# Attention's first scores and exponentials put ahead of the last in-projection block, and the gate's modulation one step later

## What is computed

```python
mod = jax.nn.silu(c) @ w_mod[l] + b_mod[l]
shift, scale, gate = jnp.split(mod, 3, axis=-1)
u = rms_norm(h, norm_w[l]) * (1.0 + scale[:, None, :]) + shift[:, None, :]
p = u @ w_in[l]
q, k, v = qk_heads(p, q_norm_w[l], k_norm_w[l])      # 8 query heads, 2 key heads of 64
k_all = jnp.concatenate([k_c, k], axis=1)            # 256 keys of the context and 512 own
attn = attend_blocked(q, k_all, v_all) * jax.nn.silu(p[..., ZA_LO:ZA_HI])
conv = conformer_conv(p[..., GLU_LO:GLU_HI], ...) * jax.nn.silu(p[..., ZC_LO:ZC_HI])
out = jnp.concatenate([attn, conv], axis=-1) @ w_out[l]
h = h + gate[:, None, :] * out
```

## Time and profile before

| | |
|---|---|
| median of 3 runs | 1076.65 us (1076.53 to 1078.28) |
| the profiled execution, its own time | 1075.98 us |
| its span, first to last instruction | 1074.2 us |
| TensorE matmul (PE) busy | 1041.7 us, 97% |
| VectorE (DVE) busy | 650.7 us, 61% |
| ScalarE (ACT) busy | 455.0 us, 42% |
| granted TensorE clock | 1.000 |
| chain that ended last | PE 76%, DVE 14%, ACT 4%, issue 3%, DMA 2% |

### The profile page before, as it was taken

How to read it: one execution, slowest core, us unless ns; L and a number is a source line. 1 busy time by engine, 2 the same in 40 slices (tenths; PEclk the granted TensorE clock), 3 DMA queues, 4 the chain that set the end, 5 groups by cost and what they waited for, 6 DMA issues and landing times.

```text
span 1074.2 us, 22576 instructions
## 1 busy us (share of the span) xinstructions
PE 1041.7 (97%) x9816; PEld 824.2 (77%) x9816; DVE 650.7 (61%) x1019; ACT 455.0 (42%) x738; POOL 5.6 (1%) x10
## 2 busy tenths in 40 slices
PE   8999998988999999999999999999999999999998
PEld 6777776776787777777777767787888888888887
DVE  4569898975457575868787757664443223444322
ACT  5354554677425543444535245344342112443111
POOL 0000000000000000000000000000000000000000
PEclk9999999999999999999999999999999999999999
DMA  9912134000522210101110121333323232333230
GB/s 362 371 60 98 59 99 174 4 2 2 196 79 99 79 41 22 42 28 37 42 41 23 42 81 42 105 111 98 97 93 105 98 98 79 98 98 105 96 104 30
DMA packets 26161, 95.01 MB, mean 88 GB/s; under 512 B 2896, under 2 KB 3152, under 8 KB 25552
## 3 DMA queue, kind: packets, MB, share of 16 engines
q1 hardware_dynamic: 26064, 93.57, 25.2%
HBM read 89.36 MB, written 4.19 MB: 87 GB/s over the span
## 4 chain that ended last, share of the span: by engine, by line
PE 76%; DVE 14%; ACT 4%; issue 3%; DMA 2%; SPq 1%; POOL 0%; ACTq 0%; DVEq 0%
PE psum L845 20%; PE psum L847 18%; PE psum L846 18%; DVE work L2037 4%; PE psum L855 3%; PE psum L1284 2%; DMA ring<-weights 2%; PE psum L1297 2%; PE psum L1053 1%; DVE small_temps L2226 1%; PE psum L1356 1%; PE psum L1333 1%; PE psum L1009 1%; PE psum L1376 1%; DVE in_weights_low L2093 1%
## 5 line engine op out<-in xcount | busy, mean ns | idle before, releaser
L2093 DVE TENSOR_TENSOR weights_low<-ring,weights_high 128x1024 fp32r<-128x1024 f32 x70 | 85.8, 1226 | 75.3 <-ACT weights_high L1647 75.3
L1647 ACT ACTIVATE weights_high<-ring 128x1024 fp32r<-128x1024 f32 x70 | 73.6, 1052 | 127.5 <-PE psum L847 127.5
L845 PE MATMUL psum<-normed_high,weights_high 128*128 128x512 f32 x256 | 100.1, 391 | 0.2 <-DVE weights_low L2093 0.2
L847 PE MATMUL psum<-normed_high,weights_low 128*128 128x512 f32 x256 | 99.7, 389 | 0.0
L846 PE MATMUL psum<-normed_low,weights_high 128*128 128x512 f32 x256 | 99.6, 389 | 0.0
L845 PE MATMUL psum<-hidden_high,weights_high 128*128 128x512 f32 x256 | 99.6, 389 | 0.0
L847 PE MATMUL psum<-hidden_high,weights_low 128*128 128x512 f32 x256 | 99.6, 389 | 0.0
L846 PE MATMUL psum<-hidden_low,weights_high 128*128 128x512 f32 x256 | 99.6, 389 | 0.0
L1617 ACT ACTIVATE work<-psum 128x384 f32<-128x384 f32 (+1 forms) x116 | 56.8, 539 | 62.3 <-PE psum L1009 20.9
L2037 DVE SCALAR_TENSOR_TENSOR work<-work,small_sb 128x512 f32<-128x512 f32 x116 | 80.0, 744 | 0.1
L845 PE MATMUL psum<-pair_normed_high,pair_weights_high 128*128 128x512 f32 x176 | 75.7, 430 | 0.8 <-DVE normed_low L2097 0.8
(11 more groups left out here) (319 smaller groups left out, 2102.7 us busy)
## 6 DMA issues: line engine op xcount, KB each, us to landing
ring<-weights SPq DMA_DIRECT2D x135, 512.0 KB, 3.7
work<-weights SPq DMA_DIRECT2D x10, 512.0 KB, 13.1
residual<-xT SPq DMA_DIRECT2D x4, 512.0 KB, 6.0
mixed<-weights SPq DMA_DIRECT2D x4, 512.0 KB, 6.2
residual_saved<-residual SPq DMA_DIRECT2D x8, 256.0 KB, 4.5
residual<-residual_saved SPq DMA_DIRECT2D x1, 2048.0 KB, 9.0
outT<-residual SPq DMA_DIRECT2D x8, 256.0 KB, 3.2
tables_sb<-tables SPq DMA_DIRECT2D x1, 1280.0 KB, 10.6
```

The source lines that it names most:

```text
L845: pe.matmul(out, wh, high(k), start=first and n == 0, stop=False)
L847: ins = pe.matmul(out, wl, high(k), start=False, stop=last and n == len(order) - 1)
L1647: act.activation(wsplit(q)[0], room_of(b), ACT.Copy).then_inc(w_high, 1)
L2093: vec.tensor_tensor(low, room_of(b), high.bitcast(F32), ALU.subtract).then_inc(w_low, 1)
```

## The change

The scores, maxima and exponentials of step 0 move ahead of block za3 in the programs of TensorE, VectorE and ScalarE. The blocks za0 to za3 get the banks 7, 4, 5 and 6, so that banks 0 to 3 are open to the scores. Since za3 still reads the normed input when the first two exponentials are written, the first two probability buffers move to the memory of the head squares and head rstd, and the other four lie in the normed input. The gate's modulation moves by one step: gate_m to steps 1 and 2, gate_t to step 4, ScalarE's copy of gate_m to the end of step 3, VectorE's reading of the columns behind the taps of step 5. The convolution's mean stays in steps 5 to 8. Cut to its core (`exp_scores`, `exp_pair`, `row_max` and `score_pair` only move up in their programs, unchanged):

```diff
-BESIDE_ATTENTION = {n: ("gate_m", 4 * n, 4 * n + 4) for n in range(DK // 4)}
-BESIDE_ATTENTION.update({3: ("gate_t", 0, DK), 10: ("cvar", 0, CK)})
+BESIDE_ATTENTION = {1 + n: ("gate_m", 4 * n, 4 * n + 4) for n in range(DK // 4)}
+BESIDE_ATTENTION.update({4: ("gate_t", 0, DK), 10: ("cvar", 0, CK)})
 BESIDE_ATTENTION.update({5 + k: ("cmean", k, k + 1) for k in range(CK)})
...
+FIRST_SCORES = f"za{NQ - 1}"
...
     for n, x in enumerate(QZ_BLOCKS):
+        if x == FIRST_SCORES:
+            scores(0)
+        if x[:2] == "za":
+            rotation[0] = (7, 4, 5, 6)[int(x[2])]
         add(x)
...
     for u in range(STEPS + VALUE_LAG):
-        if u < STEPS:
-            for h in range(2):
-                o.append((f"s{u}_{h}", 2, 2 * h))
+        if 0 < u < STEPS:
+            scores(u)
...
-        PR = [NORMED[:, n * SKEYS:(n + 1) * SKEYS] for n in range(PROBS - 1)]
-        PR.append(region(at + NQ * S, SKEYS)); at += 2 * NQ * S
+        PR = [x[:].rearrange("p a b -> p (a b)")[:, 0:SKEYS] for x in (HS, HR)]
+        PR += [NORMED[:, n * SKEYS:(n + 1) * SKEYS] for n in range(PROBS - 2)]
+        at += 2 * NQ * S
...
             for n, x in enumerate(QZ_BLOCKS):
+                if x == FIRST_SCORES:
+                    pe.wait_ge(k_low, 1)
+                    score_pair(0)
                 in_product(x, x)
...
-            pe.wait_ge(k_low, 1)
-            pe.wait_ge(*is_free("v_hi"))
...
             for u in range(STEPS + VALUE_LAG):
-                if u < STEPS:
+                if u == 0:
+                    pe.wait_ge(*is_free("v_hi"))
+                elif u < STEPS:
                     score_pair(u)
...
             for n, x in enumerate(IN_BLOCKS):
+                if x == FIRST_SCORES:
+                    for h in range(2):
+                        exp_pair(0, h)
                 for q in split_beside(n):
                     weights_high(q)
...
-                if u < STEPS:
+                if 0 < u < STEPS:
                     for h in range(2):
                         exp_pair(u, h)
                 if t >= 0:
                     turned_out(t, 1)
-                if u == 2:
+                if u == 3:
                     copy_out("gate_m", MODROW)
...
             for n, x in enumerate(IN_BLOCKS):
+                if x == FIRST_SCORES:
+                    for h in range(2):
+                        row_max(h, f"s0_{h}", SKEYS)
                 behind = split_beside(n) if n == OWN_BUFFERS else []
...
-                if u < STEPS:
+                if 0 < u < STEPS:
                     for h in range(2):
                         row_max(2 * u + h, f"s{u}_{h}", SKEYS)
...
                 if u < len(STEP_TAPS):
                     taps = convolve_on(taps, STEP_TAPS[u])
-                if u == 4:
+                if u == 5:
                     modulation_columns("gate", 2, "b_gate")
```

More of the change, by code:

```diff
@@ L287, in psum_order @@
             o.append((BESIDE_ATTENTION[u][0], 1, 7))
+    rotation[0] = None
     add(*(f"out{m}" for m in range(5)), "mem_sum", *(f"out{m}" for m in range(5, DK)))
@@ L983, in _, with score_pair @@
             in_product("v", "vx")
+            def score_pair(u):
+                j, qt = divmod(u, QT)
+                pe.wait_ge(q_low, j + 1)
+                s = [take(f"s{u}_{h}") for h in range(2)]
+                for lo, hi in ((0, S), (S, SKEYS)):
+                    for h in range(2):
+                        rows = slice(h * DH, (h + 1) * DH)
+                        at = slice(qt * P, (qt + 1) * P)
+                        pe.matmul(s[h][:, lo:hi], QHI[rows, j, at], KH[rows, lo:hi], start=True, stop=False)
+                        pe.matmul(s[h][:, lo:hi], QHI[rows, j, at], KL[rows, lo:hi], start=False, stop=False)
+                        ins = pe.matmul(s[h][:, lo:hi], QLO[rows, j, at], KH[rows, lo:hi], start=False, stop=True)
+                        if hi == SKEYS:
+                            full_inc(ins, f"s{u}_{h}")
             for n, x in enumerate(QZ_BLOCKS):
+                if x == FIRST_SCORES:
+                    pe.wait_ge(k_low, 1)
+                    score_pair(0)
                 in_product(x, x)
@@ L1055, in beside_attention @@
                     full_inc(ins, name)
-            pe.wait_ge(k_low, 1)
-            pe.wait_ge(*is_free("v_hi"))
[L1060 to L1072, removed]
-                            full_inc(ins, f"s{u}_{h}")
             def turn_probs(t, h):
@@ L1687, in first_taps, with exp_scores, exp_pair @@
                 act.activation(CTS[i % 2], GLU[:, i, 1:1 + S], ACT.Copy, scale=w[1]).then_inc(conv_begun, 1)
+            def exp_scores(i, out, name, w):
+                free_inc(act.activation(out, bank(name, w), ACT.Exp,
+                                        bias=NEGMAX[:, i % 4:i % 4 + 1],
+                                        accum_out=ROWSUM[:, i % 4:i % 4 + 1]), name)
+            def exp_pair(u, h):
+                i = 2 * u + h
+                act.wait_ge(negmax, i + 1)
+                if i >= PROBS:
+                    before = i - PROBS
+                    act.wait_ge(*is_full(f"pt{before // 2}_{before % 2}_1"))
+                exp_scores(i, PR[i % PROBS], f"s{u}_{h}", SKEYS)
             for n, x in enumerate(IN_BLOCKS):
+                if x == FIRST_SCORES:
+                    for h in range(2):
+                        exp_pair(0, h)
                 for q in split_beside(n):
@@ L2180, in convolve_on, with row_max @@
                 return at
+            def row_max(i, name, w):
+                vec.wait_ge(*is_full(name))
+                one = slice(i % 4, i % 4 + 1)
+                vec.tensor_reduce(NEGMAX[:, one], bank(name, w), AX, ALU.max, negate=True).then_inc(negmax, 1)
             taps = 0
             for n, x in enumerate(IN_BLOCKS):
+                if x == FIRST_SCORES:
+                    for h in range(2):
+                        row_max(h, f"s0_{h}", SKEYS)
                 behind = split_beside(n) if n == OWN_BUFFERS else []
@@ L2221, in _ @@
                     weights_low(q)
-            def row_max(i, name, w):
-                vec.wait_ge(*is_full(name))
-                one = slice(i % 4, i % 4 + 1)
-                vec.tensor_reduce(NEGMAX[:, one], bank(name, w), AX, ALU.max, negate=True).then_inc(negmax, 1)
             def divide(i):
```

13 lines of the change are left out of this document (2 added, 11 removed).

## The result

The changed kernel takes **1081.21 us** (median of 7 runs, 1079.33 to 1085.73) against 1076.74 us for the kernel before (7 runs, 1076.18 to 1078.42). The ratio is 1.0034 (95% interval 1.0022 to 1.0047): slower, clear of noise, by 3.7 us if taken on 1076.7. The forecast was 1078.5 us with a range of 1076.0 to 1081.0. Direction and the wait that was named are there. The ratio, taken on the 1076.65 us from which the forecast was built, gives 1080.3 us, near the range's upper end; the median itself lies just past it. Of the prediction's three cases the one with 0.31 came (slower by over 0.2%), not the one with 0.66.

A forecast was written before the change was run, and what follows sets the result against it. VectorE was taken to bound the attention steps up to 216.90 us. Terms of -0.67 us up to step 5 and +2.51 us in it summed to +1.84 us, giving 1078.5 us, range 1076.0 to 1081.0.

The forecast's parts named there:

- the one with 0.66: Whole kernel: measured time within 0.2% of the kernel before, chance 0.66.
- What bounds the stretch: VectorE, from 170.35 us to step 6's maxima: its speed sets the steps; its early waits allow at most 2.67 us gain.
- First gain: Early scores: VectorE reaches step 1's maxima 0.59 us earlier, and step 5's 0.67 us earlier.
- new wait: VectorE idles 1.75 us ahead of za3's denominator, replacing old waits of 0.97 and 1.24 us.
- The wait for bank 7: Step 5: TensorE's convolution mean waits until VectorE has read the gate's columns; +2.51 us at VectorE.
- Rival A: Step 5: the wait for bank 7 costs nothing, leaving only the gain, -0.6 us, 1076.05 us; chance 0.08.
- Level case of step 3: Step 3's maxima: scores ready at 187.81, VectorE free at 187.74; taken as VectorE's; 0.6 us if TensorE's.
- rival B: TensorE's clock falls behind idle times of 3.4 and 3.2 us; behind the second, together +4.0 us, 1080.6; chance 0.14.
- After the stretch nothing comes back: After 217 us nothing gives the loss back; out-projection starts 1.8 us later than 280.2.
- Rival C: First part gains more or later steps absorb some: +0.7 to +1.0 us, 1077.5 us; chance 0.10.

The follow-up runs named there:

- both idle times filled: The change plus filling matmuls that nobody reads, 12 in step 1 and 8 in step 5, in TensorE's two long idle times: 1081.20 us, ratio 1.0031.
- the second run: Kernel before with only step 0's scores, maxima and exponentials moved ahead of za3, the gate's modulation left in place: 1080.39 us, ratio 1.0030.
- the run with neither wait: The change with the gate's columns read behind step 4's taps and 12 unread filling matmuls in step 1: 1078.93 us, ratio 1.0014.

## Why the prediction was right or wrong

**What bounds the stretch**: right. VectorE sets it, and its waits were the place to look.

**First gain, forecast 0.59 us at step 1's maxima, 0.67 at step 5's**: right, a little small. The new wait was 1.56 us (forecast 1.75; the denominator came 3.38 us behind the first maxima where I had worked out 3.50), so step 1's maxima gained 0.72 us (178.93 - 171.17 = 7.76 us against 8.48). With both idle times filled, step 5's maxima gained 0.75 (197.70 - 170.18 = 27.52 against 28.27).

**The wait for bank 7**: right in place, cause and price. It was to cost 2.51 us at VectorE; in the run with both idle times filled, maxima of step 5 to those of step 6 take 205.43 - 197.70 = 7.73 us against 5.10 before, so 2.63. Sum +1.84 forecast, +1.88 measured there. Rival A, which needed the wait to be hidden, is refuted: TensorE waited 2.76 us with the scores of step 6 behind it.

**Level case of step 3, gate's second half in step 2**: right. VectorE did not wait ahead of step 3's maxima in the filled runs, and the transfer of blocks 6 and 7 was no longer felt. What the prediction missed is that this transfer is what forbids the early scores without the gate's move, as the second run showed.

**The clock**: this is the step that failed. The forecast's sum has no term for a fall of the clock. I had the idle times about right (3.4 and 3.2 us forecast, 3.44 and 2.76 measured), and the fall stood as rival B, with 2.2 us behind the second and 1.3 us or far more behind the first; but I gave it 0.14. It happened at both places in both profiles of the change. Its terms: maxima of step 3 lie 189.94 - 171.17 = 18.77 us into the stretch against 17.31 in the run with neither wait (187.94 - 170.63), so the first fall costs 1.46 us; from step 5's maxima to step 6's it takes 209.31 - 200.16 = 9.15 us against 7.73 with filling, so the second costs 1.42. In the change's second profile the two are 1.38 and 1.57 us. Together with the wait: -0.7 + 1.5 + 2.6 + 1.4 = +4.8 us, which is the stretch (+4.77, +4.83); the total rose by 3.7 us by the ratio and by 4.5 us from median to median. With these in, the forecast would have been 1081.4. That the range reached up to 1081.0 was for a part of rival B, so the measured time lies at its edge for a reason that the sum did not hold. The reason for my 0.14 was that the trace of before showed no idle time longer than 1.71 us, which tells nothing either way. The rule of the Trainium skill (TensorE: Matmul & The Clock Gate, Why this matters for your kernels), that idle gaps between bursts of matmuls bring the lower clock, was against the change, and the measurement agrees with it: behind 3.44 and 2.76 us of idle time the granted clock was 0.53 and 0.51. The second of these is shorter than the gap at which the page's warning begins; there the measurement decides.

**After the stretch nothing comes back**: right. The first out-projection product starts 5.61 us later in the change's profile (285.82 against 280.21), as late as step 6's maxima (5.59); 0.82 us of both is the later start of the stretch. The forecast of 1.8 us had the path right and lacked the falls. TensorE's timeline of the change:

```profile
285.82 0.79 PE L855 MATMUL psum<-gated_high,out_weights_high 128*128 128x512 f32 x1
```

**Rival C** (more gain than found): the waits could shrink, but not in this order of taps; the run with the taps moved got 1.28 us from the same stretch, within the 2.67 us bound of the earlier trace rows.

## What to carry to other kernels

When work is moved by one step, look at who frees the PSUM bank that the next result takes, and where in its queue the freeing instruction stands: here a 0.17 us instruction behind five taps kept TensorE waiting for 2.76 us. Starting a chain earlier opens idle time on TensorE where the chain is bound elsewhere, and it must be priced with the clock: in these runs each of the nine idle times of 2.58 to 3.44 us in the stretch had a fall behind it. Reorder the engine that bounds the chain so that the idle time never opens: moving two taps took the stretch from -0.35 to -1.28 us, while filling reached -0.67 at best.

## What the runs showed of the hardware that I had not expected

An idle time of TensorE of 2.58 us was followed by the lower clock; those of 1.26 us in the stretch and of up to 1.75 us at 141 us were not. A single idle time is not the whole matter: two of 1.54 and 1.33 us with 1.05 us of products between them had a fall behind them (0.50 at 184 to 186 us, in the run with only the early scores). The price of a fall differed: 1.4 to 1.6 us for each in the two profiles of the change, 2.08 us for the first with the columns read early (step 3's maxima 19.39 us into the stretch), 1.01 us for the second with the first idle time filled, and 0.32 us for the first with six gate blocks in step 1.

The kernel before shows a mean clock of 0.998 in 11 of 29 executions of one comparison; they took 1.5 us more on average than the 16 at 1.000 (1078.28 against 1076.76 us). The change's profile has such a fall late in the run, outside the change, behind short products, as this window shows (columns as in the earlier trace rows):

```profile
684.00:686.00 2.00, 2.00 (x5) 1.22 (x4) 1.20 (x3) 0.63 (x1) 0.00 (x0) 0.50 0.00 0
```

Both profiles of the kernel before have the same products with full clock, so that fall comes and goes. From the product at 633.90 us to the one at 688.69 us (first profile of before) it takes 54.8 us in the nine profiles without this fall and 56.4 or 56.5 us in the five with it, so it costs 1.6 to 1.7 us. That, 2.50 us of "issue" idle time, 0.82 us of later start and the 4.77 us of the stretch make up the 9.7 us by which the profiled execution of the change is longer than that of before.
